# Output and down projections as tokens by features, the residual kept in token rows

## The reference, cut to what matters

```python
hn = rms_norm(h_res, norm_mix_gain)              # two mixers read hn: attention a, convolution c
h_res = h_res + (gate_attn * a + gate_conv * c) @ w_out                     # output projection, 1024 x 1024
hn = rms_norm(h_res, norm_mlp_gain)              # second norm
h_res = h_res + square(relu(hn @ w_mlp_up)) @ w_mlp_down                    # 1024 x 4096, 4096 x 1024
y = rms_norm(h_res, final_norm_gain)
```

## Time and profile before

| | us |
|---|---|
| median of 3 runs | 919.56 (919.0 to 920.38) |
| the profiled execution | 917.25 |
| its span, first to last instruction | 915.2 |
| TensorE busy | 905.1 (99%) |
| VectorE busy | 620.3 (68%) |
| ScalarE busy | 450.7 (49%) |
| granted TensorE clock | 0.999 of full speed |

### The profile page before, as it was taken

How to read it: one execution, slowest core, us unless ns; L and a number is a source line. 1 busy time by engine, 2 the same in 40 slices (tenths; PEclk the granted TensorE clock), 3 DMA queues, 4 the chain that set the end, 5 groups by cost and what they waited for, 6 DMA issues and landing times.

```text
span 915.2 us, 13783 instructions
## 1 busy us (share of the span) xinstructions
PE 905.1 (99%) x5079; PEld 789.2 (86%) x5079; DVE 620.3 (68%) x963; ACT 450.7 (49%) x725; POOL 22.3 (2%) x40
## 2 busy tenths in 40 slices
PE   8999999999999999999999999999999999999997
PEld 7999998899998998888888888888888888888886
DVE  7799989999999999985756556443443344334543
ACT  6432246777777777666842344322342234115523
POOL 2010000000000000010000000000000000000000
PEclk9999999999999999999999999999999999999999
DMA  9333332212221222223335333343333333333502
GB/s 265 92 98 92 92 93 69 70 50 68 69 69 47 80 57 69 71 69 90 95 92 183 92 92 92 93 115 93 93 92 103 104 89 95 94 104 100 162 1 93
DMA packets 154043, 84.36 MB, mean 92 GB/s; under 512 B 3103, under 2 KB 151583, under 8 KB 154000
## 3 DMA queue, kind: packets, MB, share of 16 engines
q1 hardware_dynamic: 152768, 82.32, 31.3%
q10 hardware_dynamic: 640, 1.18, 0.4%
q0 software_dynamic: 592, 0.29, 0.2%
HBM read 81.62 MB, written 2.16 MB: 92 GB/s over the span
## 4 chain that ended last, share of the span: by engine, by line
PE 96%; DVE 2%; ACT 1%; DMA 1%; issue 0%; ACTq 0%; DVEq 0%
PE pj L1375 62%; PE pj L1371 17%; PE pQ L1498 3%; PE pQ L1515 3%; PE pj L1677 2%; PE pQ L1677 2%; PE pj L1413 1%; PE pQ L1485 1%; PE pQ L1484 1%; PE pQ L1518 1%; DMA u<-in_norm_mix_gain_dram 1%; PE pj L1526 0%; PE pj L1424 0%; PE pQ L1392 0%; DVE cv L1010 0%
## 5 line engine op out<-in xcount | busy, mean ns | idle before, releaser
L559 ACT ACTIVATE w_hi<-raw 128x1024 fp32r<-128x1024 f32 x129 | 135.8, 1053 | 136.6 <-PE pj L1375 108.2
L1375 PE MATMUL pj<-in_hi,w_lo 128*128 128x512 f32 x512 | 201.6, 394 | 0.0
L1375 PE MATMUL pj<-in_hi,w_hi 128*128 128x512 f32 x512 | 201.1, 393 | 0.0
L1375 PE MATMUL pj<-in_lo,w_hi 128*128 128x512 f32 x512 | 200.7, 392 | 0.0
L915 DVE TENSOR_TENSOR w_lo<-raw,w_hi 128x1024 fp32r<-128x1024 f32 x129 | 157.5, 1221 | 34.3 <-ACT w_hi L559 34.0
L1010 DVE SCALAR_TENSOR_TENSOR cv<-u,prm,cv 128x512 f32<-128x512 f32 x240 | 170.7, 745 | 0.5
L1375 PE MATMUL pj<-mid_hi,w_hi 128*128 128x512 f32 x320 | 125.7, 393 | 0.0
L1375 PE MATMUL pj<-mid_hi,w_lo 128*128 128x512 f32 x320 | 124.6, 390 | 0.0
L1375 PE MATMUL pj<-mid_lo,w_hi 128*128 128x512 f32 x320 | 124.6, 389 | 0.0
L1375 PEld LDWEIGHTS pj<-in_hi,w_hi 128*128 128x128 f32 x512 | 96.3, 188 | 20.2 <-issue 0.6
L1375 PEld LDWEIGHTS pj<-in_lo,w_hi 128*128 128x128 f32 x512 | 96.2, 188 | 18.2 <-issue 0.5
(11 more groups left out here) (202 smaller groups left out, 1144.3 us busy)
## 6 DMA issues: line engine op xcount, KB each, us to landing
raw<-in_w_in_dram SPq DMA_DIRECT2D x57, 512.0 KB, 3.8
raw<-in_w_mlp_up_dram SPq DMA_DIRECT2D x32, 512.0 KB, 4.0
raw<-in_w_mlp_down_dram SPq DMA_DIRECT2D x32, 512.0 KB, 3.6
raw<-in_w_attn_out_dram SPq DMA_DIRECT2D x8, 512.0 KB, 3.6
raw<-in_w_conv_out_dram SPq DMA_DIRECT2D x8, 512.0 KB, 3.7
raw<-in_w_out_dram SPq DMA_DIRECT2D x8, 512.0 KB, 3.6
ga<-in_x_dram SPq DMA_DIRECT2D x4, 512.0 KB, 8.2
cv<-in_x_dram SPq DMA_DIRECT2D x1, 2048.0 KB, 9.1
```

The lines of the kernel that those rows point to most:

```text
L559: A(w_hi[:, c % SPLIT, :], raw[:, c % RAW, :], ACT.Copy).then_inc(s_hi, 1)
L1375: last = mm(prod(c), wt, src[:, at:at + NT], **flags)
```

## The change

The output projection and the down projections of the first three blocks take the form of the last block's. A load is now 256 rows x 512 columns of the weight (`row_pair`, two row tiles). In `token_chunk` 128 tokens of `mid_hi` or `mid_lo` are stationary and 512 columns of weights move; for each of the load's two row tiles it goes over the four token tiles with three products each, into the four banks of `pQ`, one bank for each token tile. Four chunks give the first half of the features of all tokens, four the second half.

The residual stays in token rows in `y_tok`. VectorE adds x (output projection, `state_sum`) or the old residual (`block_sum`) when a token tile's half is done. The eight feature tiles of the new residual are turned once, by `state_transposes`, into the inner two banks of `pj` (`h_turned`): tiles 0 to 3 in the middle of chunks 4 and 5 of the output projection, 4 to 7 in the first up chunk. The second norm's sums of squares are now taken over rows by ScalarE (`state_square`), and its factor is no longer applied to the hidden value. As r is positive, square(relu(r h)) = r^2 square(relu(h)), so r^2 = 1/(mean + eps), made by `state_scale` behind the fourth hidden tile of the first block, goes as a factor of each token row into `block_sum`, and into the last block's `add_half`. The transposes of x and of the last block, the product with 1/1024, the root and the wide reciprocal are gone. The DMA of x is issued ahead of load 4 of the output projection.

```diff
@@ SyncE
+            def row_pair(w, j, row=0):
+                f, kk = divmod(j, KT // 2)
+                return w[0][ds(row + kk * (2 * P), 2 * P), ds(f * HW, HW)].rearrange("(k p) n -> p k n", p=P)
+            for j in range(KT):
+                if j == KT // 2:
+                    sp.wait_ge(s_clo, KT)
+                    sp.dma_start(x_again, x[0].rearrange("(t p) d -> p t d", p=P)).then_inc(s_again, 16)
+                load(row_pair(w_out, j), N_WO + j)
...
-                    load(columns(w_mlp_down, j * P, ds(b * D, D)), N_MLP + KT + j, b, 2 * KT)
+                    load(row_pair(w_mlp_down, j, b * D), N_MLP + KT + j, b, 2 * KT)
@@ ScalarE
-            for m in range(KT):
-                high(N_WO + m + 1)
-                act.wait_ge(s_rT, m + 1)
-                A(feat(res, m), pT6 if m % 2 == 0 else pO7, ACT.Copy).then_inc(s_res, 1)
-                act.wait_ge(s_ev, N_WO + m - N_AO + 3)
-                wait(act, s_hacc, m)
-                A(scratch(m), feat(res, m), ACT.Square).then_inc(s_hsq, 1)
-                A(feat_in(in_hi, m), feat(res, m), ACT.Copy, scale=par(R_G2, m)).then_inc(s_ghi, 1)
+            def state_square(t, f):
+                act.wait_ge(s_add, added(0, f, t))
+                wait(act, s_hss, f * QT + t)
+                A(junk[:, 0:HW], y_half(y_tok, t, f), ACT.Square,
+                  accum_out=ss[:, f * QT + t:f * QT + t + 1]).then_inc(s_hss, 1)
+            def state_high(m):
+                act.wait_ge(s_hT, m + 1)
+                A(feat_in(in_hi, m), h_turned(m), ACT.Copy, scale=par(R_G2, m)).then_inc(s_ghi, 1)
+            for j in range(KT // 2):
+                high(N_WO + j + 1)
+            high(N_WO + 5)
+            state_square(0, 0)
+            state_square(1, 0)
+            state_high(0)
+            state_high(1)
+            high(N_WO + 6)
+            state_high(2)
+            state_high(3)
+            high(N_WO + 7)
+            state_square(2, 0)
+            state_square(3, 0)
+            high(N_MLP)
+            high(N_MLP + 1)
+            for m in range(KT // 2, KT):
+                state_high(m)
+            for t in range(QT):
+                state_square(t, 1)
...
-                    if k == 0 and j == 0:
-                        act.wait_ge(s_hsum, 1)
-                        A(bc[:, 0, :], pS[:, 0:NT], ACT.Sqrt, bias=eps_rms[:, :]).then_inc(s_hsd, 1)
-                        high(c + 2)
...
-                if 1 <= j <= QT:
-                    act.wait_ge(s_resT, j)
-                    A(y_tok[:, j - 1, :], res_psum(j - 1), ACT.Copy).then_inc(s_rtok, 1)
@@ VectorE
-            V.memset(bc[:, 1, :], 0.0).then_inc(s_hacc, 1)
...
+            def tile_wait(t, f, stage, c, it=None):
+                if t < QT - 1:
+                    wait(dve, s_tile, tile_done(stage, f, t), it, 2 * (QT - 1))
+                else:
+                    wait(dve, s_mm, c + (f + 1) * KT // 2, it, 2 * KT)
+            def state_sum(t, f):
+                tile_wait(t, f, 0, N_WO)
+                V.tensor_tensor(y_half(y_tok, t, f), y_psum(t, 0), y_half(x_again, t, f), ALU.add).then_inc(s_add, 1)
+            def state_low(m):
+                dve.wait_ge(s_ghi, m + 1)
+                V.scalar_tensor_tensor(out=feat_in(in_lo, m), in0=h_turned(m), scalar=par(R_G2, m),
+                                       in1=feat_in(in_hi, m).bitcast(F32), op0=ALU.mult,
+                                       op1=ALU.subtract).then_inc(s_glo, 1)
+            for j in range(KT // 2):
+                low(N_WO + j + 1)
+            dve.wait_ge(s_again, 16)
+            for t in range(QT):
+                state_sum(t, 0)
+            low(N_WO + 5)
+            state_low(0)
+            state_low(1)
+            low(N_WO + 6)
+            state_low(2)
+            state_low(3)
+            low(N_WO + 7)
+            low(N_MLP)
+            for t in range(QT):
+                state_sum(t, 1)
+            low(N_MLP + 1)
+            for m in range(KT // 2, KT):
+                state_low(m)
...
-                    V.scalar_tensor_tensor(out=pT[:, j % 2, :], in0=prod(c), scalar=0.0, in1=bc[:, 0, :],
-                                           op0=ALU.max, op1=ALU.mult).then_inc(s_relu, 1)
+                V.tensor_scalar(pT[:, j % 2, :], prod(c), 0.0, None, ALU.max).then_inc(s_relu, 1)
...
+            def state_scale():
+                dve.wait_ge(s_hss, 2 * QT)
+                V.tensor_tensor(rsum[:, 0:QT], ss[:, 0:QT], ss[:, QT:2 * QT], ALU.add).then_inc(s_r2, 1)
+                dve.wait_ge(s_r2, 1)
+                V.tensor_scalar(rsum[:, 0:QT], rsum[:, 0:QT], 1.0 / D, RMS_EPS, ALU.mult, ALU.add).then_inc(s_r2, 1)
+                dve.wait_ge(s_r2, 2)
+                V.reciprocal(rinv[:, 0:QT], rsum[:, 0:QT]).then_inc(s_r2, 1)
+                dve.wait_ge(s_r2, 3)
+            def block_sum(t, f, psum, stage, it=None):
+                wait(dve, s_add, added(stage - 1, f, t), it, 2 * QT)
+                return V.scalar_tensor_tensor(out=y_half(y_tok, t, f), in0=psum, scalar=rinv[:, t:t + 1],
+                                              in1=y_half(y_tok, t, f), op0=ALU.mult, op1=ALU.add)
...
-                    V.tensor_tensor(feat(res, j), prod(c), feat(res, j), ALU.add).then_inc(s_acc, 1)
+                    low(c + j + 1, it, 2 * KT)
+                    if j % (KT // 2) == KT // 2 - 1:
+                        f = j // (KT // 2)
+                        for t in range(QT):
+                            tile_wait(t, f, k + 1, c, it)
+                            block_sum(t, f, y_psum(t, 0), k + 1, it).then_inc(s_add, 1)
@@ TensorE
+            def token_chunk(c, j, stage, ready, it=None, between=None):
+                f, kk = divmod(j, KT // 2)
+                wait(pe, s_lo, c + 1, it, 2 * KT)
+                for i in range(2):
+                    kt = 2 * kk + i
+                    if f == 0:
+                        ready(kt)
+                    for t in range(QT):
+                        if kt == 0 and f == 1:
+                            wait(pe, s_add, added(stage, 0, t), it, 2 * QT)
+                        elif kt == 0 and stage > 0:
+                            wait(pe, s_add, added(stage - 1, 1, t), it, 2 * QT)
+                        tok = slice(kt * NT + t * P, kt * NT + (t + 1) * P)
+                        cols = slice(i * HW, (i + 1) * HW)
+                        for n, (mid, w) in enumerate(((mid_hi, w_hi), (mid_lo, w_hi), (mid_hi, w_lo))):
+                            last = mm(y_psum(t, 0), mid[:, tok], w[:, c % SPLIT, cols],
+                                      start=kt == 0 and n == 0, stop=kt == KT - 1 and n == 2)
+                        if kt == KT - 1 and t < QT - 1:
+                            last.then_inc(s_tile, 1)
+                    if i == 0 and between is not None:
+                        between()
+                last.then_inc(s_mm, 1)
+            def state_transposes(*ms):
+                for m in ms:
+                    pe.wait_ge(s_add, added(0, m // (KT // 2), QT - 1))
+                    wait(pe, s_glo, m - 1 if m >= 2 else 0)
+                    for t in range(QT):
+                        last = nc.tensor.transpose(h_turned(m)[:, t * P:(t + 1) * P], y_tok[:, t, m * P:(m + 1) * P],
+                                                   ident[:, :])
+                    last.then_inc(s_hT, 1)
+            for j in range(KT):
+                between = {4: lambda: state_transposes(0, 1), 5: lambda: state_transposes(2, 3)}.get(j)
+                token_chunk(N_WO + j, j, 0, lambda kt: pe.wait_ge(s_mlo, kt + 1), None, between)
...
-                        pe.wait_ge(s_hacc, KT + 1)
-                        mm(pS[:, 0:NT], mean_w[:, :], bc[:, 1, :], start=True, stop=True).then_inc(s_hsum, 1)
+                        chunk(c, 0, 6, in_hi, in_lo, first=first)
+                        state_transposes(4, 5)
+                        chunk(c, 6, 12, in_hi, in_lo, first=first)
+                        state_transposes(6, 7)
+                        chunk(c, 12, total, in_hi, in_lo, first=first)
```

More of the change, by code:

```diff
@@ L296, in y_half, with h_turned, tile_done, added @@
             return buf[:, t, f * HW:(f + 1) * HW]
-        def res_psum(t):
-            return pQ[:, t % 2 * D:(t % 2 + 1) * D]
+        def h_turned(m):
+            return pj[:, 0, 512:1024] if m % 2 == 0 else pj[:, 1, 0:512]
+        def tile_done(stage, f, t):
+            return 2 * (QT - 1) * stage + (QT - 1) * f + t + 1
+        def added(stage, f, t):
+            return 2 * QT * stage + QT * f + t + 1
         def in_cols(buf, t):
@@ L469, in _ @@
                     load(columns(w_in, it * (4 * P) + (O_GC + j * P)), N_GC + j, it)
[L470 to L474, removed]
+            for first, w in ((N_AO, w_attn_out), (N_CO, w_conv_out)):
                 with sp.Fori(0, KT // 4) as it:
@@ L848, in mlp @@
                     c = N_MLP + 2 * KT * k + j
[L849 removed]
+                    if not (k == 0 and j == 0):
```

(39 more changed lines are left out.)

95 lines of the change are left out of this document (28 added, 67 removed).

## The result

The changed kernel takes 913.51 us (median of 7 runs, 912.94 to 916.37), beside 919.0 us for the kernel before on the same chip. The ratio is 0.995, with a 95% interval of 0.9937 to 0.9962. A second timing on another occasion gave 0.9946 (0.9933 to 0.9959). The change is worth about half a per cent: the interval allows a gain of 3.5 to 5.8 us. The two medians by themselves are 5.5 us apart, a ratio of 0.9940. The prediction was 915.5 us, a ratio of 0.9956 to the 919.56 us that it started from, with a range of 913.8 to 917.7.

The account below looks back on a forecast made before the run. TensorE's unbroken chain of instructions was taken as the bound. Terms -8.38 + 3.65 + 0.3 + 0.29 + 0.06 = -4.08 us took the profiled 917.25 to 913.2 and the median 919.56 to 915.5 us, range 913.8 to 917.7.

Parts of the forecast that it names:

- The products, taken at no change: Output projection and three looped blocks' down projections: turned operands and banks alternating every three products cost 0.
- Rival B: Turned stages' 768 products cost more when banks change; 5.3 ns each takes the whole gain; chance 0.04 beyond the old time.
- C: Rival: the clock falls in the turned stages; 2.4% of products at 1.2 GHz eat the gain; chance 0.04.
- The increments on single tiles: Turned stages: extra increments for three token tiles at each half's end, 6 a stage, 24 in all, cost 0.
- Removed, -8.38 us: TensorE loses 32 transposes of x (3.86), 32 of the last block's residual (3.65) and the product with means (0.87).
- Added, +3.65: TensorE gains 32 transposes of the new residual, four groups of eight at 0.91 us, in output projection and first up chunk.
- Wait (1): Between column halves TensorE reuses four banks that VectorE's sums must free: at least 1.1 us to spare, cost 0.
- Wait (2): Start of the up projection: transposes wait for VectorE's differences; 0.3 us taken, ends 0 and 1.5 us.
- Wait (3): First up chunk: ScalarE's four squares behind the copies delay the hidden chunk and weight splits; cost 0, but thin.
- Wait (4): Last block's up chunks 4 and 6 wait for w_lo, 2 x 0.29 in place of 0.29: +0.29 us.
- The tail, +0.06: Behind the last product, the last sum takes a factor: 0.75 in place of 0.69 us.
- The table load: Square root's table load moves to the tail's first root: cost 0, or 1.28 us if it hit the last root.

Follow-up runs that it names:

- both fixes: Changed kernel with last block's w_lo split ahead of the down projection's and feature tiles 6 and 7 turned into two other free banks: 913.56 us, ratio 0.9948.
- the first fix: Changed kernel with only the last block's order of splits turned: 395.33 us from the output projection's start to the last product, 0.62 below the changed kernel.

## Why the prediction was right

Right in direction and in mechanism. In size it is right by the stretch (4.24 us against 4.14) and by the ratio (0.995 against 0.9956). As a time, 915.5 us is 2.0 us too high: 913.51 lies 0.3 us under the lower end of the range, and the 5.5 us between the medians are more than the 5.2 that bounded the forecast. By its own steps:

- *The products, taken at no change.* Held exactly: 43.52 us for a stage of 192 in either form, and no price for a change of bank in three arrangements. Rival B is out, and C with it, as the granted clock is 1.00 in every stretch from 420 us on in the run that alternates with each product. The Trainium skill's section on the clock that the prediction names for C ("A second HAM failure mode: psum-queue depth-cycling", in "TensorE: Matmul & The Clock Gate") puts its kernel's oscillation down to short idle times between groups of matmuls, not to the change of bank alone; in this run TensorE lost 1.75 us between products at a change of halves, and the stage's granted clock stayed at 1.00. One subtraction in this step was wrong: from 512 to 264 columns are 248, not 252, which is 0.43 ns a column. The split into a part for columns and a fixed part doesn't bear that, and the runs with other arrangements of banks decide the point without it. The increments on single tiles cost nothing either: 192 products with six more of them take what 192 without take. The Trainium skill, "TensorE: Matmul & The Clock Gate", section "The cost: per-tile semaphore tail", gives 26.3 ns for each, for small matmuls that are packed as tiles into the array. As an estimate from it that would have been 0.16 us a stage, and it does not show here, where the increments are 0.68 us apart.
- *Removed, -8.38 us.* Leaving out both turns gave -7.10 where -7.22 (7.51 less 0.29) was worked out; the product with the means, put back, costs 0.91 at its place where 0.87 was taken.
- *Added, +3.65.* Eight transposes put back cost 0.90 on average: 3.30 + 0.29 = 3.59 for four groups.
- *Wait (1), the sums between the halves, at 0.* Right as to the time. The room was given as at least 1.1 us and is 0.95. The reckoning compared the sum's end with the product's start; the weight load of that product, ahead by 0.2, is what waits, and half of a short wait of it (0.21 us late, 0.11 lost) is still hidden.
- *Wait (2), the start of the up projection, 0.3.* It is 0.25. In the chain above the second four transposes begin 0.51 us after the first four instead of 0.44, and by the timeline the second product after them comes 1.35 us behind their first, where 1.10 is normal. The difference of tile 5 ends at 558.95, which is 4.36 us behind the output projection's last product (554.59) where 4.35 was drawn. Taking the wait away (both fixes less the first fix alone: 395.33 to 395.13) gave 0.20.

```profile
557.54 1.41 DVE L1299 SCALAR_TENSOR_TENSOR in_lo<-pj,prm,in_hi 128x512 fp32r<-128x512 f32 x2
```

- *Wait (3), ScalarE's squares, at 0.* Nothing waits. VectorE's split for the third up chunk ends 12.3 us behind T, the start of the last product of the output projection (12.5 was worked out, 12.9 is the limit); its row of the timeline is

```profile
565.67 1.23 DVE L940 TENSOR_TENSOR w_lo<-raw,w_hi 128x1024 fp32r<-128x1024 f32 x1 [0.26 <-ACT w_hi L568]
```

- *Wait (4), the last block, 2 x 0.29.* Two waits at chunks 4 and 6, as drawn, none at 5 and 7. The first fix shows their size (0.62 to 0.67 for both), the transposes put back show their cause: with the old cover back at chunks 1 to 4 one of them goes.

```profile
839.93 0.19 PEld L1435 LDWEIGHTS pj<-in_hi,w_hi 128*128 128x128 f32 x1 [0.44 <-DVE w_lo L947]
...
851.12 0.19 PEld L1435 LDWEIGHTS pj<-in_hi,w_hi 128*128 128x128 f32 x1 [0.43 <-DVE w_lo L947]
```

- *The tail, +0.06.* 0.76 in place of 0.70 on the chain. The table load did no harm.
- *The sum.* -4.14 ahead of the tail, -4.24 measured. The term that was off is the last one, the step from the profiled execution to the median. The profiled execution before lay 2.3 us under the median of the three runs shown, and I carried that difference over. After, the profiled execution lies on the median. It was the spread of single executions, and no property of the kernel: the profiled execution before (917.25) was as quick as the quickest of the 18 that the two timings hold (917.21). With the change of 4.1 us taken off the later median of 919.0 the forecast would have been 914.9. The other 1.4 us down to 913.51 are inside the interval of the ratio, and no trace shows a gain that would account for them. The range had a slip of its own: with no new wait the sum is -4.67; the -5.0 of its lower end also takes away the wait that was there before.

## What to carry to other kernels

When TensorE is the unbroken chain, count its instructions at the spacing of their starts and leave the other engines' busy times alone; that gave 4.1 of 4.2 us here, while ScalarE and VectorE lost 15 us of work that bought nothing. Taking instructions out of the bottleneck also takes away the cover of whatever ran beside them: look for the stretch where another engine's turn (5.79 us) is longer than the shortened stage (5.44), and turn its order so that what the bottleneck waits for comes first. Count a margin up to the weight load, which is ahead of the product by 0.2 us here, and test it by putting in a delay of known length; a transposed product form is free only as long as its tiles end as far apart as the other engine needs to drain them.

## What was not expected

The time ahead of the change moves more between executions than the change's smaller terms: the output projection began at 509.02, 509.48, 510.12, 509.11 and 510.93 us in five executions. All of it arises in the first 22 us: from the start of the piece of 64 products there (19.69, 20.25, 20.99, 19.92 and 21.82 us) to the output projection are 489.1 to 489.3 us in each. In the first four the chain of waits starts with the DMA of the first norm's gain on ScalarE's queue, which landed 4.7, 5.0, 6.0 and 4.7 us after its issue. In the fifth, the version with both fixes, the gain took 5.4, but the chain starts with the load of x, and a piece of 24 products takes 4.42 us where the other four take 3.12 to 3.15:

```profile
1.66 6.76 DMA ga<-in_x_dram
...
14.67 4.42 PE pj L1477 x24
```

The granted clock is 0.57 from 10 to 18 us there and 1.00 in the same stretch of the changed kernel:

```profile
10.00:18.00 8.00, 7.71 (x43) 6.86 (x42) 7.17 (x10) 6.49 (x11) 0.00 (x0) 0.57 1.13 325
```

So the start of an execution differs by when its first loads land and, in the fifth, by a lower clock. The whole times fit this without proving it: where the mean granted clock is on record, the slowest executions of a version (916.37 us of the changed kernel, 920.46 twice of the kernel before, 915.57 of the version with both fixes) are those with the lowest one, 0.993 or 0.994. Why the clock is lower in some stays open. A difference under 1 us between two versions of this kernel can be read from a stretch of the trace, not from its time.
